# Gated short convolution layer on one core: the output projection of the convolved part as block products

## The reference, cut to what matters

```python
h = rms_norm(x, pre_norm)                      # x (4096, 1024)
proj = h @ w_in                                # 1024 -> 3*1024 + 1536 + 512
b, c, u = three columns of 1024; gate = proj[..., 3072:4608]; q = the last 512
z = c * u
mix = b * (conv[0] * z[t-2] + conv[1] * z[t-1] + conv[2] * z[t])
k, v = split(rms_norm(mem, mem_norm) @ w_mem_kv)   # mem (256, 1024), 4 heads of 128
mem_o = softmax(q k^T / sqrt(128)) v               # every frame attends to all 256
y = (concat(mix, mem_o) * silu(gate)) @ w_out      # (1536) -> 1024
x = x + rms_norm(y, post_norm)
```

## Time and profile before

| | |
|---|---|
| device time, median of 3 runs | 2373.96 us (2372.81 to 2376.64) |
| the profiled execution | 2373.23 us, span 2371.5 us |
| TensorE busy | 2237.3 us, 94% |
| VectorE, ACT, POOL busy | 1110.3, 711.0, 60.9 us |
| mean granted TensorE clock | 0.975 |
| 16 DMA engines | 188 GB/s on average |

### The profile page before, as it was taken

How to read it: one execution, slowest core, us unless ns; L and a number is a source line. 1 busy time by engine, 2 the same in 40 slices (tenths; PEclk the granted TensorE clock), 3 DMA queues, 4 the chain that set the end, 5 groups by cost and what they waited for, 6 DMA issues and landing times.

```text
span 2371.5 us, 26241 instructions
## 1 busy us (share of the span) xinstructions
PE 2237.3 (94%) x10074; PEld 1851.6 (78%) x10074; DVE 1110.3 (47%) x1735; ACT 711.0 (30%) x1257; POOL 60.9 (3%) x108
## 2 busy tenths in 40 slices
PE   3899999999999999999999999997489999999997
PEld 2687878788888888888888888776378888888886
DVE  8577776713552243444351353231544444444531
ACT  4333433411211131221131121111444444444430
POOL 0000000000000000000000000000000000000000
PEclk9899999999999999999999999999599999999999
DMA  4686666777566677666577655547323333333321
GB/s 153 236 310 242 250 251 244 265 258 249 194 205 213 219 246 254 227 207 213 193 242 256 208 196 182 207 166 246 122 80 107 107 107 107 107 107 107 107 76 53
DMA packets 158235, 445.82 MB, mean 188 GB/s; under 512 B 13952, under 2 KB 46752, under 8 KB 155936
## 3 DMA queue, kind: packets, MB, share of 16 engines
q1 hardware_dynamic: 139984, 376.49, 46.3%
q0 software_dynamic: 18128, 67.66, 8.4%
HBM read 320.36 MB, written 123.73 MB: 187 GB/s over the span
## 4 chain that ended last, share of the span: by engine, by line
PE 85%; DVE 8%; DMA 3%; issue 2%; ACT 1%; SPq 0%; DVEq 0%; POOL 0%; ACTq 0%; POOLq 0%
PE banks L1162 28%; PE banks L1163 28%; PE banks L1164 28%; DVE hop_lo L811 2%; DMA slots<-w_split 2%; PE banks L1282 1%; DVE x_in L789 1%; DVE x_in L807 1%; DVE slots L841 1%; DMA q_raw<-q_kept 1%; DMA x_in<-in_x_t 0%; DVE wo_lo L1055 0%; DVE st_w L835 0%; DVE acc L784 0%; DMA conv_raw<-g_kept 0%
## 5 line engine op out<-in xcount | busy, mean ns | idle before, releaser
L1162 PE MATMUL banks<-hop_hi,slots 128*128 128x512 f32 x2240 | 882.7, 394 | 50.3 <-DVE hop_lo L811 22.3
L1163 PE MATMUL banks<-hop_lo,slots 128*128 128x512 f32 x2240 | 877.1, 392 | 0.0
L1164 PE MATMUL banks<-hop_hi,slots 128*128 128x512 f32 x2240 | 876.7, 391 | 0.0
L1162 PEld LDWEIGHTS banks<-hop_hi,slots 128*128 128x128 f32 x2240 | 424.0, 189 | 147.5 <-issue 43.7
L1164 PEld LDWEIGHTS banks<-hop_hi,slots 128*128 128x128 f32 x2240 | 423.8, 189 | 89.3
L1163 PEld LDWEIGHTS banks<-hop_lo,slots 128*128 128x128 f32 x2240 | 424.0, 189 | 88.7 <-issue 1.4
L1162 PE MATMUL banks<-wo_hi,gc_hi 128*128 128x512 f32 x512 | 202.6, 396 | 0.0
L1163 PE MATMUL banks<-wo_lo,gc_hi 128*128 128x512 f32 x512 | 199.9, 391 | 0.0
L1164 PE MATMUL banks<-wo_hi,gc_lo 128*128 128x512 f32 x512 | 199.7, 390 | 0.0
L886 DVE TENSOR_TENSOR u<-banks,u 128x512 f32<-128x512 f32 x56 | 38.7, 690 | 297.4 <-PE banks L1164 297.4
L579 ACT ACTIVATE s<-banks 128x512 f32<-128x512 f32 x80 | 47.8, 598 | 416.7 <-PE banks L1164 416.7
(11 more groups left out here) (137 smaller groups left out, 2344.7 us busy)
## 6 DMA issues: line engine op xcount, KB each, us to landing
slots<-w_split SPq DMA_DIRECT2D x420, 512.0 KB, 3.4
w_split<-slots SPq DMA_DIRECT2D x140, 512.0 KB, 2.9
raws<-in_w_in SPq DMA_DIRECT2D x80, 256.0 KB, 3.9
x_in<-in_x_t SPq DMA_DIRECT2D x16, 1024.0 KB, 6.9
g_kept<-mix POOLq DMA_DIRECT2D x16, 1024.0 KB, 6.6
x_res<-in_x POOLq DMA_DIRECT2D x32, 512.0 KB, 5.0
conv_raw<-g_kept SPq DMA_DIRECT2D x32, 512.0 KB, 4.6
out_x<-x_res POOLq DMA_DIRECT2D x32, 512.0 KB, 3.4
```

What stands on the lines that cost most here:

```text
L1162: nc.tensor.matmul(dst, a, c, start=first, stop=False, skip_group_check=True)
L1163: nc.tensor.matmul(dst, a, d, start=False, stop=False, skip_group_check=True)
L1164: return nc.tensor.matmul(dst, b, c, start=False, stop=last, skip_group_check=True)
```

## The change

The convolved part of the output projection becomes a fifth round (`OUT`) of 7-for-8 block products. Its right operands are made from `w_conv` (the first 1024 rows of w_out, loaded into `x_in`), its units from 128-token columns of `g_kept` (4 raw blocks of 256 KB for each of 16 pairs of 128-token row blocks, now 512 B pieces in two transfers a group). All 112 units are built on ACT and VectorE 4 steps ahead, the first four beside pair 19 of macro 3. The sums of a pair (256 tokens x 1024 outputs) go from `mix` to `y_kept` in HBM. Keys and values are made four pairs earlier (behind pairs 6 to 13), kept in HBM while `w_conv` takes their place, and brought back at step 2 of the round. Attention stands beside the block products, a head in 3 steps from step 6: scores after step a, weighing of the head before after a+1, transposes after a+2; the gated result goes to `mem_kept`. Last come 32 row blocks of 24 matmuls with memory's 512 rows of w_out (`w_mem`), to which `sum_up` adds the kept sums; then square, root, scale, residual, each 1024 wide. The core of the diff:

```diff
+OUT = MACROS
+OUT_PAIRS = NT * SUB // 2
+OUT_UNITS = OUT_PAIRS * PRODUCTS
+OUT_X_AFTER = {16: (0, 1), 17: (2, 3)}
+HEADS = NT * MH
+FIRST_SCORE = 6
 KV_BLOCKS = 2 * MH
-KV_AFTER = [3 * PAIRS + 10 + b for b in range(KV_BLOCKS)]
+KV_AFTER = [3 * PAIRS + 6 + b for b in range(KV_BLOCKS)]
...
+        YP = 4
+        y_sum = at("y_sum", X_AT + 16 * KB, [YP, D])
+        x_res = at("x_res", Z_AT, [2, D])
+        junk = at("junk", M_AT, [D])
...
+                    if i in OUT_X_AFTER and m + 1 == MACROS:
+                        sp.wait_ge(kv_kept_dma, 16 * 4)
+                        for n in OUT_X_AFTER[i]:
+                            load_x(n, OUT)
+                    if i == max(OUT_X_AFTER) and m + 1 == MACROS:
+                        sp.wait_ge(w_lo, UNITS0 + 2 * KV_BLOCKS)
+                        for x in (X11, X21, X22, X12):
+                            load_raw(ALL_PAIRS, x)
...
+            for step in range(-SLOTS, OUT_UNITS):
+                pair, r = divmod(step + SLOTS, PRODUCTS)
+                if r == R1 and pair + 1 < OUT_PAIRS:
+                    load_raw(ALL_PAIRS + pair + 1, X11)
+                    load_raw(ALL_PAIRS + pair + 1, X21)
+                if r == R3 and pair + 1 < OUT_PAIRS:
+                    load_raw(ALL_PAIRS + pair + 1, X22)
+                    load_raw(ALL_PAIRS + pair + 1, X12)
+                if step == 2:
+                    sp.wait_ge(hop_lo_done, (OUT + 1) * PRODUCTS)
+                    for n, part in enumerate((k_hi, k_lo, v_hi, v_lo)):
+                        sp.dma_start(flat(part[:].bitcast(f32)), kv_kept[n]).then_inc(kv_back_dma, 16)
+                    load_q(0)
+                    load_m(0)
+                n, phase = divmod(step - FIRST_SCORE, 3)
+                if phase == 0 and 0 < n + 1 < HEADS and step >= FIRST_SCORE:
+                    load_q(n + 1)
+                if phase == 0 and 0 <= n - 1 and n < HEADS:
+                    load_m(n)
+                if step == OUT_UNITS - 11:
+                    load_mem(0)
+                    load_mem(1)
+                if step == OUT_UNITS - 7:
+                    sp.wait_ge(pv_done, HEADS)
+                    sp.dma_start(flat(x_in[:, 0, :, :]), w_mem).then_inc(w_mem_dma, 16)
+                    for n in range(2, CHUNKS):
+                        load_mem(n)
+            for n in range(NT * SUB):
+                load_y(n)
+                if n + CHUNKS < NT * SUB:
+                    load_mem(n + CHUNKS)
...
+            for step in range(OUT_UNITS):
+                pair, r = divmod(step, PRODUCTS)
+                if r == R1 and pair:
+                    keep_sums(ALL_PAIRS + pair - 1)
+                n, phase = divmod(step - FIRST_SCORE - 6, 3)
+                if phase == 0 and 0 <= n < HEADS:
+                    t, h = divmod(n, MH)
+                    pool.wait_ge(mem_gated, n + 1)
+                    pool.dma_start(mem_kept[t * SUB:(t + 1) * SUB, :, h, :].rearrange("s p n -> p s n"),
+                                   gated_mem[:, n % 2, :].rearrange("p (s n) -> p s n", n=P)).then_inc(mem_kept_dma[n % 2], 16)
...
+            for step in range(OUT_UNITS):
+                pair, r = divmod(step, PRODUCTS)
+                n, phase = divmod(step - FIRST_SCORE, 3)
+                if phase == 1 and 0 <= n + 1 < HEADS:
+                    query(n + 1)
+                if phase == 1 and 0 <= n < HEADS:
+                    soften(n)
+                if phase == 0 and 0 <= n - 1 < HEADS:
+                    turned(n - 1)
+                evacuate(ALL_PAIRS + pair, r)
+                ahead(OUT, step)
+                if step == R5:
+                    operand_hi(OUT, R4)
+                if pair == OUT_PAIRS - 1 and r in (R6, R3):
...
+            for step in range(OUT_UNITS):
+                pair, r = divmod(step, PRODUCTS)
+                n, phase = divmod(step - FIRST_SCORE, 3)
+                if phase == 2:
+                    if 0 <= n - 1 < HEADS:
+                        gate(n - 1)
+                    if 0 <= n < HEADS:
+                        soften(n)
+                    if 0 <= n + 1 < HEADS:
+                        query(n + 1)
+                if phase == 0 and 0 <= n - 1 < HEADS:
+                    turned(n - 1)
+                if phase == 1 and 0 <= n < HEADS:
+                    row_maxima(n)
+                if step == R1:
+                    operand_lo(OUT, R2)
+                    token_sum(OUT, 3)
+                if step == R5:
+                    operand_lo(OUT, R4)
+                ahead(OUT, step)
+                if r in (R3, R7, R2):
+                    add(ALL_PAIRS + pair, r)
+                if pair == OUT_PAIRS - 1 and r in (R7, R4):
+                    operand_lo(OUT + 1, R1 if r == R7 else R5)
...
+            def sum_up(n):
+                dve.wait_ge(unit_done, MEM_UNIT[n] + 1)
+                dve.wait_ge(y_dma[n % YP], 16 * (n // YP + 1))
+                y = y_sum[:, n % YP, :]
+                nc.vector.tensor_tensor(y, both_banks(n), y, ALU.add).then_inc(y_summed, 1)
...
+            for n in range(NT * SUB):
+                sum_up(n)
+                if n + SLOTS < NT * SUB:
+                    mem_unit_lo(n + SLOTS)
+                if n:
+                    finish(n - 1)
...
+            for step in range(OUT_UNITS):
+                pair, r = divmod(step, PRODUCTS)
+                multiply(ALL_PAIRS + pair, r)
+                n, phase = divmod(step - FIRST_SCORE, 3)
+                if phase == 0 and 0 <= n < HEADS:
+                    score(n)
+                if phase == 1 and 0 <= n - 1 < HEADS:
+                    weigh(n - 1)
+                if phase == 2 and 0 <= n < HEADS:
+                    turn(n)
+
```

More of the change, by code:

```diff
@@ L64, with kind_of, built_pair, trunk @@
         LOADS[_u] = sum(1 for v in LOADS if v % SLOTS == _u % SLOTS) + 1
+def kind_of(p):
+    return KINDS[p % PAIRS] if p < ALL_PAIRS else "y"
 def count(kinds, p):
-    return sum(KINDS[n % PAIRS] in kinds for n in range(p))
-def trunk(nc, x, x_t, mem, in_gains, post_g, conv, w_in, w_kv, w_out, out):
+    return sum(kind_of(n) in kinds for n in range(p))
+def built_pair(p):
+    return p if p < PAIRS else PAIRS + p - ALL_PAIRS
+def trunk(nc, x, x_t, mem, in_gains, post_g, conv, w_in, w_kv, w_conv, w_mem, out):
     f32 = mybir.dt.float32
@@ L431, in _, with load_y @@
[L431 to L451, removed]
-                if step >= 0 and step % 2 == 0 and 4 + step // 2 < NT * SUB:
-                    load_conv(4 + step // 2)
+            def load_y(n):
+                if n >= YP:
+                    sp.wait_ge(y_final, n - YP + 1)
+                sp.wait_ge(y_kept_dma, 16 * (n // 2 + 1))
+                sp.dma_start(y_sum[:, n % YP, :], y_kept[n // 2][:, n % 2 * D:(n % 2 + 1) * D]).then_inc(y_dma[n % YP], 16)
@@ L772, in _ @@
+                nc.scalar.activation(ysd[:, n % 2:n % 2 + 1], ysq[:, n % 2, 0:1], ACT.Sqrt, scale=1.0 / D,
+                                     bias=eps[:]).then_inc(ysd_done, 1)
         @block.vector
@@ L1002, in _ @@
                         token_sum(0, 3)
-                    if m == 0:
-                        build(step + SLOTS)
-                    if m + 1 < MACROS and i == PAIRS - 1:
+                    ahead(m, step)
+                    if i == PAIRS - 1:
                         if r in (R5, R6, R7, R2, R4):
@@ new lines, in finish @@
+                nc.vector.scalar_tensor_tensor(out=y, in0=y, scalar=yrs[:, one], in1=post_gain[:],
+                                               op0=ALU.mult, op1=ALU.mult).then_inc(y_scaled, 1)
+                dve.wait_ge(x_res_dma[n % 2], 16 * (n // 2 + 1))
+                dve.wait_ge(y_scaled, n + 1)
+                nc.vector.tensor_tensor(row, y, row, ALU.add).then_inc(y_final, 1)
+            dve.wait_ge(post_dma, 16)
+            for n in range(NT * SUB):
+                sum_up(n)
+                if n + SLOTS < NT * SUB:
+                    mem_unit_lo(n + SLOTS)
+                if n:
+                    finish(n - 1)
@@ new lines, in _ @@
+            for n in range(NT * SUB):
+                unit_ready(MEM_UNIT[n])
+                if n == 0:
+                    pe.wait_ge(exp_done, HEADS * SUB)
+                elif n == 1:
+                    pe.wait_ge(mem_gated, HEADS)
+                elif n == 2:
+                    pe.wait_ge(copied, count("qcy", LAST_PAIR) + 1)
+                    pe.wait_ge(c22_done, LAST_PAIR + 1)
+                elif n == 3:
+                    pe.wait_ge(c12_done, LAST_PAIR + 1)
+                    pe.wait_ge(c11_done, LAST_PAIR + 1)
+                else:
+                    pe.wait_ge(y_summed, n - 3)
+                for half in range(2):
+                    if n == 0:
+                        pe.wait_ge(hop_lo_done, (OUT + 1) * PRODUCTS + half + 1)
+                    for k in range(MH):
+                        g = [a[:, k * P:(k + 1) * P] for a in unit(MEM_UNIT[n])]
```

(3 more changed lines are left out.)

492 lines of the change are left out of this document (217 added, 275 removed).

## The result

The changed kernel takes 2443.6 us (median of 4 runs, 2440.55 to 2448.57), the kernel before beside it 2375.25 (4 runs): a ratio of 1.029, interval 1.027 to 1.031. I had said 2341, and faster at 0.76. It is slower, and outside the range. The profiled execution took 2442.7 us; its span is 2440.9 where 2339.0 were forecast, 101.9 more.

What follows compares the result with a forecast made beforehand. TensorE's matmul stream plus one gap was taken as the bound; 2259.5 without new waits plus 6 + 1 + 5.1 + 10 + 22 + 24 + 1.4 + 10 gave a 2339.0 span, 2341 us executed; range 2303 to 2392.

Steps and rivals of the forecast that it cites:

- The passage: Between projection and output stage: the serial start's 70.3 us go, as new-round loads and units overlap projection pair 19.
- the matmuls: Output stage on TensorE: convolved part falls from 1536 to 1344 matmuls, 599.1 us in all, 43.5 less.
- The boundary: From projection into the new round: four units ahead of token_sum 3 on VectorE make the wait 5.1 us.
- The first head: Start of attention: late q holds ACT, then VectorE's sum for R4; 8 us plus 2 for the clock, bounds 3 to 14.
- Into memory's rows: Entry to the last stage: hop_lo for half 1 comes behind the last evacuation and unit, 1.4 us.
- Loads at the end of the projection: w_conv and raw loads delay units, 6 us (0 to 10); g_kept's small-piece writes, 1 us (0 to 8).
- Heads beside block products: In each head, transposes wait 0.7 us for the softmax; 22 us over 32 heads, bounds 0 and 60.
- q in SP's order: In the heads, q loads stand behind waiting raw loads and land late; 24 us in all, bounds 10 and 40.
- rival D: In the heads, TensorE's clock falls again and again; 96 us come back, 2395 to 2420 in all, chance 0.06.
- memory's rows: Last stage: x_res round trip makes a row block 5.65 us; 10 us over 174.1, bounds 0 and 50.
- Rival C: Memory's rows bound by x_res's round trip, 6.5 to 7.0 us per block; 2365 to 2382 in all, chance 0.11.
- Rivals E and F: E: stall of 3 us or more in every head, 2390 to 2420, 0.06; F: passage stays, near 2385, 0.03.

Runs made afterwards that it cites:

- the best version: Changed kernel plus six x_res buffers, earlier q loads, soften right behind row_maxima, and load_q(0) ahead of keys and values: 2282.1 us, ratio 0.962.
- q first: Changed kernel with load_q(n+2) ahead of the raw loads one step earlier, in place of load_q(n+1) behind them: 2400.9 us, ratio 1.011.
- six buffers: Changed kernel with six x_res buffers in place of two, x(n+3) loaded after out(n): 2359.8 us, ratio 0.9945.
- the last two runs: Changed kernel without x loads after the first two, 2356.0 us; changed kernel without kept-sum loads after the first four, 2382.1 us.

## Why the prediction was wrong

**Right.** *The passage* went, and *the matmuls* are 192 fewer: the best version gains 91.9 us over the kernel before, against 70.3 + 43.5 - 1.8 = 112 for these terms. Of the other 20, 4.7 are lost before its new round starts and 10.1 are TensorE's waits behind 1653 (the rows shown, 1.4 for hop_lo and 1.0 for v_lo); some 5 I can't put to a row. *The boundary*: 5.1 said, 3.95 measured, TensorE waiting for ACT's u. *The first head*: 8 said, 6.00 measured, for VectorE's sum, as said. *Into memory's rows*: 1.4 said, 1.42 measured. These rows of the changed kernel are the answer to the earlier trace rows:

```profile
1668.75 0.77 PE L1252 MATMUL banks<-hop_hi,slots 128*128 128x512 f32 x1 [3.95 <-ACT u L705]
...
1681.99 0.76 PE L1252 MATMUL banks<-hop_hi,slots 128*128 128x512 f32 x1 [6.00 <-DVE mix L990]
...
2172.56 0.50 PE L1252 MATMUL banks<-hop_hi,slots 128*128 128x512 f32 x1 [1.42 <-DVE hop_lo L905]
```

*Loads at the end of the projection*: 6 and 1 said, 8.8 measured. TensorE's waits for units from 1240 on are 12.7 us in 8 (9.5 in 8 before), one of them new, 2.88 at 1611.4; the clock from 1600 to 1640 was 0.91, 3.6 us lost; and 1.03 went for a sum of VectorE's at 1650.9.

**Right in kind, too small.** *Heads beside block products*: 0.7 per head said, 0.7 to 1.0 in most heads whose q is in time, 27 in all with q first, for 22. *q in SP's order*: 24 said, 28.3 measured as what goes with q first. Both lie within their bounds. *The clock*: I gave 2 us at the first head. In the heads it cost 12, and around the first head about 6: an estimate, 0.20 x 35 = 7 for the window from 1665, less what fell into the waits. What rival D described did happen, in six of the 32 heads, but its 96 us were far too much. The Trainium skill, "TensorE: Matmul & The Clock Gate", section HAM oscillation, describes a loop with a wait for a transfer in each turn, behind which each burst begins slow. The trace agrees behind the 5 us gap above (T in 1.97 and a clock of 0.82), and shows none of it behind the waits of about 1 us in the other heads. The sum of what can be named in the round, over the forecast: 9 us of T's waits (55.4 for 22 + 24), 12 + 4 of clock, 3 for a period of 11.99 where 11.9 was counted, less 3 at the boundary and first head: 25 of the 31.3. The other 6 I can't put to a row.

**Wrong: memory's rows.** The step that failed is this one: "x_res has two buffers: add to out issue 0.3, 3.2 to the next issue, 5.0 to landing, 1.3 add: 9.8 for two blocks where 10.9 are there. Loaded, out should take 1.5 more: 11.3, or 5.65 each. I take 10 over 174.1". A block took 7.92 where these 10 us made it (174.1 + 10) / 32 = 5.75: 67 us = 31 x (7.92 - 5.75), twice the whole gain that I forecast.

What was mis-sized are the landings. From out's issue to the next issue I had 4.7, and it took 7.3 + 0.3; for x I had 5.0, and it took 6.4. The prediction's own loop, with these two put in, gives 7.8 a block: some 60 of the 67 us. Both figures came from a quiet stage, the 3.2 even from its last blocks; no row stood behind the 1.5 for the load. With x loaded by SP the landings were what I had assumed (5.2 and 4.7), and a block took 6.05 for my 5.65.

The rest is POOL's order, which the prediction had left out: load_residual(n+2) waits for out(n)'s landing, and out(n+1) stands behind it. The changed kernel shows it, POOL and VectorE each in order of time:

```profile
2249.43 0.53 POOL L586 DMA_DIRECT2D x_res<-in_x  x1 [7.04 <-DMA out_x<-x_res]
2249.96 0.53 POOL L596 DMA_DIRECT2D out_x<-x_res  x1
2258.43 0.53 POOL L586 DMA_DIRECT2D x_res<-in_x  x1 [7.94 <-DMA out_x<-x_res]
2258.96 0.53 POOL L596 DMA_DIRECT2D out_x<-x_res  x1
2266.01 0.53 POOL L586 DMA_DIRECT2D x_res<-in_x  x1 [6.52 <-DMA out_x<-x_res]
...
2247.91 1.23 DVE L1237 TENSOR_TENSOR x_res<-y_sum,x_res 128x1024 f32<-128x1024 f32 x1 [3.75 <-DMA x_res<-in_x]
```

The write goes out the moment the load is issued, with no wait of its own. This loop is one landing and 0.8 (0.28 to the issue and 0.53 for it), 8.1. But the wait that it adds is short: the data of the write at 2249.96 was ready at 2249.14 (VectorE's add), 0.8 us before, and where nothing stands in front of it (six buffers, or x by SP) a write follows its data by 0.3. So the order held each write back by 0.5 us, 0.25 a block in a round trip of two: some 8 us, an estimate. With the landing that I had taken, 4.4 to 4.9, its loop would have been 5.7 at most, and this term would have held. In the kernel before the order was the same, but a head of 20 us held one block, so a wait of 2.63 cost nothing.

Why the landings grew from 3.4 and 5.0 to 7.3 and 6.4 is seen in part only: they are long where loads are issued just ahead (the last two runs). The order has a share in it, for it sends a load and a write out 0.53 us apart; how large a share no run shows. With six buffers the question loses its price: 7.4 and 8.5 cost nothing there.

Rival C named the mechanism, the round trip of x_res, and priced it at 6.5 to 7.0 per block, too low by the same landings. Rivals E and F did not occur: the long wait is in two heads of seven, not in all. The Trainium skill, "DMA: Bandwidth & Descriptors", section Bandwidth, has 425 GB/s for transfers of 16 MB, by which the 10 would have been 0. For rate alone six buffers agree, nothing was lost there; their mean was 338 GB/s over 100 us, and 424 the most in a slice of 2.75 us.

Of the signs named ahead, the three that would make the prediction wrong all came: a period of 14.15 (above 14), 7.92 per block (above 6.2), and a granted clock below 1.0 behind the first head (0.97 from 1700 to 2050).

## What to carry to other kernels

When a stage is made several times denser, price each loop over a buffer anew, with every landing in it doubled, and see whether it still fits: a landing time read from a quiet stage is no price for a busy one. If it doesn't fit, give the buffers more depth before asking why the landings are long; here the depth alone made them cost nothing. List for each in-order queue what stands behind each wait, for a wait for a queue's own last write makes the next write follow it. And before trusting a steady wait of under a microsecond on the bounding engine, look at which of the other engine's instructions could simply stand elsewhere: in the heads the order, not the work, was at fault both times.

## What the runs showed of the hardware

A 512 KB write landed in 3.4 us in the quiet stage, in 5.1 to 5.2 with either of two streams of loads beside it, and in 7.3 with both, at a DMA share of only 0.67. With both streams but x issued by SP it landed in 5.2, at 0.86 and 296 GB/s: in 6.8 to 8.1 with x and y issued in the 3 us ahead of it, in 3.2 to 3.8 with nothing issued around it. With six buffers the share was 0.96 at 338 GB/s and it landed in 7.4. So its landing followed the neighbours in time and not the mean share or rate. That is read from one trace and wasn't tested by a run of its own.

A gap of TensorE's does not always lower its clock. All nine gaps of 4.9 to 5.6 us ahead of T, five in the passage before and four in the changed kernel's heads, left T slow (1.72 to 1.97 us, for 1.09 at full clock). Shorter ones went either way: 1.97 behind a gap of 2.84, but 1.10 behind one of 3.80:

```profile
1766.03 1.10 PE L1374 MATMUL banks<-ident,probs 128*128 128x128 f32 x8 [3.80 <-DVE probs L1175]
...
1965.89 1.97 PE L1374 MATMUL banks<-ident,probs 128*128 128x128 f32 x8 [2.84 <-DVE probs L1175]
```

Which gaps cost the clock stays open.
